# Odd mixer: gate, gelu halves and token mixing ahead of the attention units; rows of three output panels between the units

## The reference, cut to what matters

```python
def odd_mixer(x, w_in, sgu_norm, sgu_w, sgu_b, fox_bf, w_out):
    p = x @ w_in                                   # 1024 -> z 1024, q k v 512 each, f 8
    z, q, k, v, f = split(p)
    z = gelu(z)
    u, g = split(z, 2)                             # 512 each
    yc = u * (tril(w_s) @ rmsnorm(g per head) + b) # tokens mixed in chunks of 128, 8 heads
    yd = forgetting_attention(q, k, v, f)          # 8 heads of 64, causal softmax
    return concat([yc, yd]) @ w_out                # 1024 -> 1024

h = h + odd_mixer(rmsnorm(h)); h = h + conv_glu_ffn(rmsnorm(h))
```

## Time and profile before

| | us |
|---|---|
| median of three runs | 1141.74 |
| profiled execution, device time | 1140.99 |
| its span | 1139.2 |
| PE busy | 1053.7 |
| DVE busy | 716.9 |
| ACT busy | 601.2 |

### The profile page before, as it was taken

How to read it: one execution, slowest core, us unless ns; L and a number is a source line. 1 busy time by engine, 2 the same in 40 slices (tenths; PEclk the granted TensorE clock), 3 DMA queues, 4 the chain that set the end, 5 groups by cost and what they waited for, 6 DMA issues and landing times.

```text
span 1139.2 us, 21429 instructions
## 1 busy us (share of the span) xinstructions
PE 1053.7 (92%) x9017; PEld 993.2 (87%) x9017; DVE 716.9 (63%) x1080; ACT 601.2 (53%) x876; POOL 5.0 (0%) x13
## 2 busy tenths in 40 slices
PE   5999787999998887999999999999899899999997
PEld 5998766899995876998999999999878799999996
DVE  6746556567557365578667767666754559666574
ACT  5543565466535554476646545445644456545543
POOL 1000000000000000000000000000000000000000
PEclk9999899999999999999999999999988899999999
DMA  8553512254646121275444655555363235555531
GB/s 281 158 144 113 158 63 75 75 168 129 190 116 200 60 75 38 80 253 157 149 150 147 212 180 178 183 180 167 104 205 99 75 111 185 185 184 184 184 111 38
DMA packets 144748, 163.59 MB, mean 144 GB/s; under 512 B 6072, under 2 KB 135552, under 8 KB 144672
## 3 DMA queue, kind: packets, MB, share of 16 engines
q1 hardware_dynamic: 143752, 161.04, 44.2%
q10 hardware_dynamic: 632, 1.30, 0.3%
q0 software_dynamic: 288, 0.14, 0.1%
HBM read 161.43 MB, written 1.05 MB: 143 GB/s over the span
## 4 chain that ended last, share of the span: by engine, by line
PE 68%; DVE 14%; ACT 11%; issue 4%; DMA 2%; SPq 1%; DVEq 0%; ACTq 0%
PE ps L440 20%; PE ps L441 19%; PE ps L442 19%; DVE panels_low L1682 4%; ACT panels_high L1163 4%; ACT probs L1149 2%; PE ps L458 2%; PE ps L530 1%; DMA panels<-in_w_in 1%; DVE neg_max L1705 1%; DVE squares L1646 1%; DVE probs L1721 1%; PE ps L661 1%; ACT unscaled L1149 1%; PE ps L568 1%
## 5 line engine op out<-in xcount | busy, mean ns | idle before, releaser
L1682 DVE TENSOR_TENSOR panels_low<-panels,panels_high 128x2048 fp32r<-128x2048 f32 (+1 forms) x146 | 329.8, 2264 | 273.6 <-ACT panels_high L1163 273.5
L440 PE MATMUL ps<-input_high,panels_low 128*128 128x256 f32 x1600 | 464.9, 291 | 28.9 <-DVE input_low L1677 7.8
L441 PE MATMUL ps<-input_low,panels_high 128*128 128x256 f32 x1600 | 457.3, 286 | 0.0
L442 PE MATMUL ps<-input_high,panels_high 128*128 128x256 f32 x1600 | 457.0, 286 | 0.0
L1163 ACT CAST panels_high<-panels 128x2048 fp32r<-128x2048 f32 (+1 forms) x146 | 274.2, 1881 | 143.3 <-PE ps L442 116.9
L440 PEld LDWEIGHTS ps<-input_high,panels_low 128*128 128x128 f32 x1600 | 311.4, 195 | 35.1 <-issue 14.5
L441 PEld LDWEIGHTS ps<-input_low,panels_high 128*128 128x128 f32 x1600 | 311.8, 195 | 0.3
L442 PEld LDWEIGHTS ps<-input_high,panels_high 128*128 128x128 f32 x1600 | 311.5, 195 | 0.0
L440 PE MATMUL ps<-ffn_hidden_high,panels_low 128*128 128x256 f32 x352 | 99.5, 283 | 6.6 <-DVE ffn_hidden_low L2208 3.8
L441 PE MATMUL ps<-ffn_hidden_low,panels_high 128*128 128x256 f32 x352 | 99.5, 283 | 0.0
L442 PE MATMUL ps<-ffn_hidden_high,panels_high 128*128 128x256 f32 x352 | 99.4, 282 | 0.0
(11 more groups left out here) (284 smaller groups left out, 1329.5 us busy)
## 6 DMA issues: line engine op xcount, KB each, us to landing
panels<-in_ffn_up SPq DMA_DIRECT2D x44, 1024.0 KB, 5.1
panels<-in_w_in SPq DMA_DIRECT2D x32, 1024.0 KB, 5.8
panels<-in_ffn_down SPq DMA_DIRECT2D x22, 1024.0 KB, 4.9
panels<-in_mix_w_in SPq DMA_DIRECT2D x20, 1024.0 KB, 5.4
panels<-in_w_out SPq DMA_DIRECT2D x8, 1024.0 KB, 5.2
panels<-in_w_pg SPq DMA_DIRECT2D x8, 1024.0 KB, 5.3
panels<-in_mix_w_out SPq DMA_DIRECT2D x8, 1024.0 KB, 6.9
panels<-in_w_pp SPq DMA_DIRECT2D x2, 1024.0 KB, 4.8
```

Source lines behind the costliest of these rows:

```text
L440: pe.matmul(dst, w[1], x[0], start=start, stop=False if not kw else True, **kw)
L441: pe.matmul(dst, w[0], x[1], start=False, stop=False if not kw else True, **kw)
L442: return pe.matmul(dst, w[0], x[0], start=False, stop=stop, **kw)
L1682: V.tensor_tensor(low_slots[slot][:, 0:size], raw[n % SLOTS][:, 0:size], high_slots[slot][:, 0:size].bitcast(F32), ALU.subtract).then_inc( ...
```

## The change

The panels are loaded in the order zg, zu, fv instead of fv, zg, zu. On PE the zg panels take the place of fv in front of the units, followed by the `wt` transposes (banks 7 and 2) and both zu panels (banks 5 and 6). Units 0 and 1 follow at once; the token mixing (banks 6 and 7) and the fv panels (banks 0 and 1) stand between unit 1's scores and the turning of unit 0. Gelu of zu is taken from PSUM by halves. In the gaps of units 1, 2 and 3 stand the first half of the rows (k 0 to 3) of output panels wo0, wo1 and wo2, in banks 0, 3 and 4; the rest of their rows (k 4, 5, then 6, 7) comes behind unit 3, and wo3 whole after that. DVE and ACT get the steps `mixed` and `fo` to split Y in quarters as they are ready. The next norm's sums 0 to 2 stand together behind wo3.

```diff
 ODD_PANELS += [(f"{name}{h}", "mix1_w_in_2", c0 + 256 * h, 256) for name, c0 in
-               (("fv", 2048), ("zg", 512), ("zu", 0)) for h in range(2)]
+               (("zg", 512), ("zu", 0), ("fv", 2048)) for h in range(2)]
...
-                    tokens(["fv0", "fv1"], 5, [("fv0", L), ("fv1", L)])
+                    tokens(["zg0", "zg1"], 0, [("zg0", L), ("zg1", L)])
+                    todo(("zg",))
+                    pe.wait_ge(sgu_landed, 16)
+                    for g in range(2):
+                        begin(f"wt{g}", (7, 2)[g])
...
+                    todo(("wt",))
+                    for g in range(2):
+                        two_chunks(f"zu{g}", 5 + g, (f"zu{g}", L))
+                        todo(("zu", g))
+                    todo(("zg_norm",))
                     pe.wait_ge(forget_ready, 1)
                     drained(pe, "fq1")
                     drained(pe, "fk1")
-                    drained(pe, "fv1")
...
+                    out_banks = (0, 3, 4, 5)
+
+                    def output_rows(g, ks):
+                        key, b = (f"wo{g}", L), out_banks[g]
+                        if ks[0] == 0:
+                            begin(f"wm_{l}_{g}", b)
+                            split(key)
+                        for j in range(2):
+                            for k in ks:
+                                pe.wait_ge(y_ready, 4 * L + k // 2 + 1)
+                                ins = product3(...)
+                        if ks[-1] == ND - 1:
+                            done(f"wm_{l}_{g}", ins)
+                            release(key)
 
                     unit(0)
                     for u in range(4):
                         todo(("normalise", u))
                         if u < 3:
                             unit(u + 1)
                         if u == 0:
...
                             pe.wait_ge(sgu_ready, 1)
                             drained(pe, "wt1")
                             mix_tokens(0)
                             mix_tokens(1)
-                        if u > 0:
+                            tokens(["fv0", "fv1"], 0, [("fv0", L), ("fv1", L)])
+                            todo(("fv",))
+                        else:
+                            output_rows(u - 1, range(0, 4))
                             weigh(u - 1)
                         turn("f", u, pidx + u)
                         todo(("turned", u))
                         if u == 0:
-                            todo(("zg_norm",))
+                            todo(("mixed",))
+                    for g in range(2):
+                        output_rows(g, range(4, 6))
                     weigh(3)
-                    normed_last[nidx] = "zu1"
+                    output_rows(2, range(4, 6))
+                    for g in range(3):
+                        output_rows(g, range(6, 8))
+                    normed_last[nidx] = "fv1"
                 nidx += 1
-                output(f"wm_{l}_", L, 2)
+                if l == 0:
+                    output(f"wm_{l}_", L, 2)
+                else:
+                    two_chunks(f"wm_{l}_3", out_banks[3], ("wo3", L))
+                    norm_sum(nidx, 2, (0, 1, 2))
...
                         elif step == "zu":
                             g = arg[0]
-                            copy_out(f"zu{g}", SG[:, g * 512:(g + 1) * 512], bank(f"zu{g}")[:, :])
-                        elif step == "sg0":
-                            drained(act, "zu1")
-                            f(SG[:, :], SG[:, :], ACT.Gelu_apprx_tanh).then_inc(act_part, 1)
+                            full(act, f"zu{g}")
+                            f(SG[:, g * 512:(g + 1) * 512], bank(f"zu{g}")[:, :],
+                              ACT.Gelu_apprx_tanh).then_inc(free(f"zu{g}"), 1)
                         split_high(place)
-                    mixed_high(DEPTH + l, ["fo0", "fo1"])
```

More of the change, by code:

```diff
@@ L992, in mix_tokens @@
                     def mix_tokens(g):
-                        b = 2 + g
+                        b = 6 + g
                         begin(f"sg{g}", b)
@@ L1007, in weigh @@
                     def weigh(u):
+                        b = 1 + u // 2
+                        if u == 0:
+                            drained(pe, "fv1")
                         if u % 2 == 0:
-                            begin(f"fo{u // 2}", 1 - u // 2)
+                            begin(f"fo{u // 2}", b)
                         values("f", u, pidx + u, lambda n, r: vh[:, n, (2 * u + r) * 64:(2 * u + r + 1) * 64],
-                               ps[1 - u // 2][:, (u % 2) * T:(u % 2 + 1) * T], True,
+                               ps[b][:, (u % 2) * T:(u % 2 + 1) * T], True,
                                close=f"fo{u // 2}" if u % 2 == 1 else None)
+                        if u % 2 == 1:
+                            todo(("fo", u // 2))
+                    out_banks = (0, 3, 4, 5)
[7 more added lines that the diff above has]
+                                pe.wait_ge(y_ready, 4 * L + k // 2 + 1)
+                                ins = product3(ps[b][:, j * T:(j + 1) * T], [t[:, k, j * P:(j + 1) * P] for t in parts(key)],
+                                               (xh3[:, k, :], xl3[:, k, :]), k == 0 and j == 0, True,
+                                               skip_group_check=True)
+                        if ks[-1] == ND - 1:
+                            done(f"wm_{l}_{g}", ins)
+                            release(key)
                     unit(0)
@@ L1021, in _ @@
                         if u == 0:
[L1022 to L1036, removed]
                             pe.wait_ge(sgu_ready, 1)
@@ L1503, in _ @@
                     f(SS[0:8, :], SS[0:8, :], ACT.Ln, bias=EPSC[0:8, 1:2]).then_inc(act_part, 1)
-                    for n in range(NT):
-                        copy_out(f"fv{n}", vh[:, n, :], bank(f"fv{n}")[:, :])
-                        split_after(f"fv{n}")
                     for place, step, *arg in agenda[DEPTH + l]:
@@ L1518, in _ @@
                             f(NZ[:, :], QN[:, :], ACT.Square).then_inc(act_part, 1)
+                        elif step == "fv":
+                            for n in range(NT):
+                                copy_out(f"fv{n}", vh[:, n, :], bank(f"fv{n}")[:, :])
+                        elif step == "mixed":
+                            mixed_high(DEPTH + l, None, (0, 1))
+                        elif step == "fo":
+                            mixed_high(DEPTH + l, ["fo0", "fo1"], (2 + arg[0],))
+                        elif step == "zg_norm":
                             log_exp()
-                        elif step == "zg_norm":
                             act.wait_ge(dve_part, 4)
@@ L2141, in _ @@
                             ins.then_inc(free(kind), 1)
-                        split_low(place)
[L2143 to L2153, removed]
+                            if g == 1:
+                                drained(dve, "sg1")
+                                drained(dve, "zu1")
+                                for i in range(2):
+                                    s = slice(i * 512, (i + 1) * 512)
+                                    V.tensor_tensor(Y[:, s], HZ[:, s], SG[:, s], ALU.mult).then_inc(yf_ready, 1)
+                        elif kind == "mixed":
+                            mixed_low(DEPTH + l, 0)
+                            mixed_low(DEPTH + l, 1)
+                        elif kind == "fo":
+                            g = arg[0]
+                            full(dve, f"fo{g}")
+                            V.tensor_copy(Y[:, 1024 + g * 512:1024 + (g + 1) * 512],
+                                          bank(f"fo{g}")[:, :]).then_inc(free(f"fo{g}"), 1)
+                            mixed_low(DEPTH + l, 2 + g)
+                        split_low(place)
                 nidx += 1
```

7 lines of the change are left out of this document (5 added, 2 removed).

## The result

The change is slower. Its median over 20 runs is 1150.45 us (1145.15 to 1154.05), that of the kernel before, on the same chip, 1142.71 (20 runs, 1140.63 to 1145.24): ratio 1.0063, 95% interval 1.0052 to 1.0074. The profiled execution took 1146.83 against 1140.99. So there are two numbers to explain: 5.8 us between the profiled executions, and about 7.2 (0.0063 of 1142) between many runs.

What follows compares the result with a forecast made beforehand. The end of the first output product, then DVE and ACT turns of 7.0 us, were taken as the bound. Terms 1.8 + 1.1 + 0.8 = 3.7 us took 1140.99 to 1144.7; 0.75 more gave median 1145.4, range 1139.5 to 1150.

Steps and rivals of the forecast that it cites:

- The case forecast: Odd mixer to feed-forward start: waits move, clock is lost, tail stays fixed; 3.7 us slower, median 1145.4, chance 0.46.
- Wait for zu0: Behind zg, PE waits for zu0's cast and low part: 6.1 us, so zu0 starts at 850.1.
- zu0 and zu1: The two zu panels resume at lowered clock after the pause, losing 1.5 us, and end at 863.5.
- Before the mixing: Ahead of token mixing, PE waits 0.9 us for gelu, wo0's cast and low part, and the scaling of zg.
- Before the first rows: Behind unit 2, PE waits 2.2 us for Y's first quarter, queued after wo2's cast and low part.
- First output product and clock in the middle: First output product ends 1.8 us late; a clock fall around 883.6 to 889.3, as likely as not, adds 1.1.
- Tail: From first add to feed-forward start stays 20.5 us, set by DVE and ACT turns of 7.0 us.
- The rival in which PE sets it: Between first add and feed-forward start, the turn contracts and PE bounds it: 6.7 us faster, 1135.0; chance 0.12.
- Its condition, a turn under 6.4: Behind the first output product, the change becomes faster rather than slower once each add-to-add turn is under 6.4 us.
- Clock at the feed-forward start: Feed-forward part starts at half clock, losing 1.5 to 3.0 us less 1.43 of slack: 0.8 taken.
- clock falls twice more: Clock falls in units 0 and 1 and the mixing, slowing fv's start: 2 to 4 us more, 1148.5; chance 0.17.

Runs made afterwards that it cites:

- the first edit: The changed kernel with zu0's cast and low part put ahead of zg's gelu; median 1141.10 us, ratio 0.9999 to the kernel before.
- the second edit: The changed kernel with the split of Y's first half put ahead of wo2's cast and low part; median 1144.10 us, ratio 1.0024 to the kernel before.
- fillers before zu0: The changed kernel with 44 unread bf16 matmuls on constants in PE's wait ahead of zu0; median 1148.10 us, ratio 1.0050 to the kernel before.
- the tail's order: The changed kernel with ACT casting the next panel before waiting for the add, odd layer only; median 1139.28 us, ratio 0.9978 to the kernel before.
- all three together: The changed kernel with zu0's cast early, Y split ahead of wo2, and tail casts ahead of the adds; median 1127.33 us, ratio 0.9865 to before.

## Why the prediction was right, point by point

**Size.** Forecast was +3.7 by profile and 1145.4 for the median. From zg to the end it is +4.7 in each of four profiled executions; another 1.1 of the first comparison lies ahead of zg (0.96, 833.20 against 832.24) and around the span (0.14). The median of the first 20 runs is 5 us above the forecast and just above the range's upper end of 1150.0; that of all 28 is 1149.2, and the ratio times the 1141.74 on record is 1148.9, both inside it. The case forecast (waits move, clock lost, tail fixed) is the one that came, but 3.7 is only half of the 7.2 of many runs. The other half is mostly the upper group of times, for which the working has no term. That the range holds the result all the same is in part luck.

**Wait for zu0.** Said: 6.1 behind zg, start at 850.1. Shifted by the 0.96 of zg's start, it starts at 850.01. The working by list order and durations held to 0.1 us, and the first edit shows that it was the largest part of the loss.

**zu0 and zu1.** Said 13.4 with 1.5 of clock; 13.22, against 11.75 where nothing waits: 1.47.

**Before the mixing.** Said 0.9; 0.57, since zu1 ended 0.3 earlier than worked out and the links behind it run closer than the sum of their durations. The Trainium skill ("ScalarE: Activation LUTs", What ACT_TABLE_LOAD costs) has a drain in addition to the load; here the next function starts 1.30 after the load's start (866.63 and 867.93), and the mixing came earlier than worked out, not later. The trace disagrees with a drain at this place.

**Before the first rows.** Said 2.2; 2.15, for `input_low`, with wo2's low part ahead of it on DVE (the second edit took both away).

**First output product and clock in the middle.** Said 1.8 + 1.1 = 2.9 for the first add. In the first profile it is 2.78; in the other three 4.24, where the first rows run at 0.50 all through (5.11 instead of 3.14: 2.0). So of the 1.1 taken for the clock, 1.0 to 2.4 came if the 1.8 was right. "As likely as not" looks too low, since four of four lost clock there.

**Tail.** Said 20.5 behind the first add; 20.44 to 20.54. PE's two waits in it, said about 3.5 each, are 3.57 and 3.19. The rival in which PE sets it did not come. Its condition, a turn under 6.4, was well put, and its price of 6.7 was close: when the cast no longer waits for the add, the turns are 5.0 and 3.59 and the tail is 7.8 shorter.

**Clock at the feed-forward start.** Said 0.8, as 1.5 to 3.0 lost less the slack of 1.43. Lost were 1.5 (the first 30 matmuls take 5.32 where the kernel before takes 3.83), and the slack took nearly all of it: before, PE waits 1.43 at 955.61, while the change has no wait there.

```profile
940.45:970.00 29.55, 29.53 (x244) 29.25 (x243) 26.75 (x42) 20.77 (x28) 0.00 (x0) 1.00 0.50 160
```

So this term was too large: about 0.1 came, the lower end of its own range. Two profiles of the experiments confirm it. With Y's order and with the fillers before zu0 the first 30 matmuls run at full clock, and from the feed-forward start to the end it still takes 209.8, as in the first profile, with the same fall near the end. What stands in this term's place is not in the working at all: 0.5 in the last 11 us of the program in each of the four profiles, and in the first one the fall of 1.5 at 1124. The sum of 3.7 is within 1.0 of the 4.7 partly because the term that was too large stood in for what was missing.

**What the working didn't have.** The upper group of times. The forecast took the one difference of before, median less profiled execution (0.75), for the change as well, while there it is 2 to 5 us. In terms of the prediction it is nearest to the rival "clock falls twice more" (1148.5): the mean clock is 0.961 to 0.967 in those runs. Where PE loses it was not seen, because no profiled execution fell there. The experiments narrow it: the group is absent or thin in every variant that fills or removes one of the waits. A mean clock of 0.967 or less stands at 0 of 12 runs with zu0's cast earlier, 0 of 12 with the tail's order, 0 of 5 with fillers before zu0, and 2 of 12 with Y's order, the two at 1149. That fits a clock that falls once more where several waits follow each other, but this is argued, not shown.

A rival is that a part of it lies ahead of the mixer. Three profiles of the experiments (the tail's order, fillers before zu0, all three together) have falls of the clock that the four of the change lack, in code that is the same in every kernel, and reach zg at 836.53, 834.10 and 835.49. The rows show two such stretches in the tail's order; in the four profiles of the change both run at 1.00.

```profile
300.00:320.00 20.00, 18.14 (x279) 17.36 (x279) 10.57 (x15) 7.14 (x7) 0.00 (x0) 0.91 0.43 130
800.00:812.00 12.00, 8.89 (x52) 8.26 (x52) 7.07 (x13) 8.30 (x14) 0.00 (x0) 0.86 0.33 90
```

Two of the three are the slowest runs of their kernel (1143.32 against a median of 1139.28, 1129.92 against 1127.33). Against it as the whole cause stands that the kernel before has the same code there, and only 3 of its 73 runs took more than 1144.

**Rows.** The prediction had no term for whether rows pay. With the old tail the adds come at the same 7.0 us with rows and without, so all that rows can save is what moves the first add: 0.9 to 2.3 us by the profiles (83.82 without them), while by the runs they cost 4.1, and that difference is open. With the tail free they are worth 9.1 us.

## What to carry to other kernels

Work moved ahead on the bottleneck engine paid here only once the chain behind it could run ahead too: look at the fixed turn of the next stage first, and at what stands in front of each cast in the helper engines' in-order lists. Two of the three places were casts that need only a landed panel but stood behind an instruction that waits for a product; in the third, such a cast stood in front of a split that PE needed sooner. Together they cost 22.6 us: the change, which brought in two of them, was slower by 7.2, and with all three re-ordered it is faster by 15.4. The same order can be harmless: in the kernel before, the tail's place was worth 0.5 us, within the noise. Compare profiled executions between fixed marks of the program, since what lies ahead of them varies by more than the effect, and look at the single times before using their median.

## What the runs showed of the hardware

The same units ran at either clock. Without rows they stayed at 0.50 (1.2 GHz) for 17.7 us, with PE busy for 14.36 of them; between dense rows they stayed at 1.00 (2.4 GHz) for 26.85 us. The Trainium skill ("TensorE: Matmul & The Clock Gate", Part 1) says that activity releases the throttled state. The stretch with rows agrees; by the sentence alone the one without rows would have regained the clock too, and it did not.

Constant bf16 matmuls in a wait keep the clock for what follows (11.75 instead of 13.22 us for 96 matmuls, 5.98 instead of 7.46 to 8.24 for 48), yet the total didn't fall by that: the clock fell later in one case, and in the other nobody waited for what was gained.

One kernel had two groups of times, with means of 1146.6 and 1152.2, with all instructions the same, and four profiled executions showed one of them only.
